# Causal attentions in tile order 3, 0, 2, 1, branch behind branch, the compressed branch folded into them, and finer waits at four stages

## What is computed

```python
def mla_mix(...):           # 12 heads, causal over 512 tokens
    s = einsum('bhqd,bhkd->bhqk', qb, k) * scale
    p = masked_softmax(s, key_pos <= tq);  o = einsum(p, v)
def nsa_mix(...):           # 12 heads in 2 groups, three branches
    s_c = einsum(qb, kc) * scale - m * dist_c        # 31 compressed keys
    p_c = masked_softmax(s_c, cmp_end <= tq);  o_c = einsum(p_c, vc)
    ...                     # o_s: top 16 of 8 blocks, so all of them; o_w: window of 512
    o = g0 * o_c + g1 * o_s + g2 * o_w               # g = sigmoid(gates)
def memory_attention(...):  # softmax over 256 memory positions
x = layer_norm(DN_ALPHA * x + concat([o_tok, o_mem]) @ w_out, ...)
```

## Time and profile before

| | |
|---|---|
| median of 3 runs | 3133.34 us (3130.97 to 3135.99) |
| the profiled execution's own time | 3133.84 us |
| its span, first to last instruction | 3132.0 us |
| mean granted TensorE clock | 0.985 |
| PE busy | 3007.3 us, 96% |
| DVE, ACT, POOL busy | 1258.7, 1072.1, 159.1 us |
| chain that ended last | PE 86%, DVE 8%, ACT 3%, issue 2% |

### The profile page before, as it was taken

How to read it: one execution, slowest core, us unless ns; L and a number is a source line. 1 busy time by engine, 2 the same in 40 slices (tenths; PEclk the granted TensorE clock), 3 DMA queues, 4 the chain that set the end, 5 groups by cost and what they waited for, 6 DMA issues and landing times.

```text
span 3132.0 us, 36507 instructions
## 1 busy us (share of the span) xinstructions
PE 3007.3 (96%) x15462; PEld 2505.1 (80%) x15462; DVE 1258.7 (40%) x1802; ACT 1072.1 (34%) x1856; POOL 159.1 (5%) x187
## 2 busy tenths in 40 slices
PE   8999999999999899999899999899999978999998
PEld 6888888888888788888668888788888855688887
DVE  3464344333335533325554322332332548543323
ACT  3323244443444322213653222212231227623221
POOL 1000000030001000001000000100000114000000
PEclk9999999999999999999999999999999969999999
DMA  5333232232221222223112332432322420023222
GB/s 198 124 105 95 99 102 77 85 89 88 74 87 49 94 94 94 94 96 114 43 42 81 95 108 94 110 108 93 96 94 94 118 53 2 28 94 94 94 96 80
DMA packets 135010, 280.06 MB, mean 89 GB/s; under 512 B 20378, under 2 KB 33098, under 8 KB 134720
## 3 DMA queue, kind: packets, MB, share of 16 engines
q1 hardware_dynamic: 125232, 247.17, 24.5%
q0 software_dynamic: 9616, 30.57, 3.2%
HBM read 271.30 MB, written 4.25 MB: 88 GB/s over the span
## 4 chain that ended last, share of the span: by engine, by line
PE 86%; DVE 8%; ACT 3%; issue 2%; DMA 1%; POOL 1%; SPq 0%; POOLq 0%; DVEq 0%; ACTq 0%
PE bank L535 24%; PE bank L537 24%; PE bank L536 23%; PE bank L691 2%; PE bank L670 2%; PE bank L546 1%; PE bank L548 1%; PE bank L549 1%; PE bank L724 1%; PE bank L743 1%; PE bank L732 1%; DVE n_p L1714 1%; PE bank L679 1%; DVE w_low L1530 1%; PE bank L651 1%
## 5 line engine op out<-in xcount | busy, mean ns | idle before, releaser
L1530 DVE TENSOR_TENSOR w_low<-raw,w_high 128x2048 fp32r<-128x2048 f32 (+3 forms) x214 | 483.8, 2261 | 1250.0 <-ACT w_high L1145 1243.7
L535 PE MATMUL bank<-xt_high,w_high 128*128 128x512 f32 x1984 | 779.1, 393 | 3.6 <-DVE w_low L1530 3.2
L537 PE MATMUL bank<-xt_high,w_low 128*128 128x512 f32 x1984 | 773.4, 390 | 0.0
L536 PE MATMUL bank<-xt_low,w_high 128*128 128x512 f32 x1984 | 772.7, 389 | 0.0
L1145 ACT ACTIVATE w_high<-raw 128x2048 fp32r<-128x2048 f32 (+3 forms) x214 | 404.1, 1888 | 933.8 <-PE bank L537 933.8
L535 PEld LDWEIGHTS bank<-xt_high,w_high 128*128 128x128 f32 x1984 | 372.2, 188 | 80.5 <-DVE w_low L1530 3.7
L537 PEld LDWEIGHTS bank<-xt_high,w_low 128*128 128x128 f32 x1984 | 372.1, 188 | 79.4
L536 PEld LDWEIGHTS bank<-xt_low,w_high 128*128 128x128 f32 x1984 | 372.4, 188 | 76.7
L535 PE MATMUL bank<-w_high,hidden_high 128*128 128x512 f32 x656 | 256.2, 391 | 3.1 <-DVE gate_rows L1899 3.1
L536 PE MATMUL bank<-w_low,hidden_high 128*128 128x512 f32 x656 | 255.5, 390 | 0.0
L537 PE MATMUL bank<-w_high,hidden_low 128*128 128x512 f32 x656 | 255.4, 389 | 0.0
(11 more groups left out here) (353 smaller groups left out, 4017.7 us busy)
## 6 DMA issues: line engine op xcount, KB each, us to landing
raw<-in_ffn_w_gu SPq DMA_DIRECT2D x80, 1024.0 KB, 5.1
raw<-in_ffn_w_down SPq DMA_DIRECT2D x44, 1024.0 KB, 5.0
raw<-in_b_w_in SPq DMA_DIRECT2D x40, 1024.0 KB, 5.1
raw<-in_a_w_in SPq DMA_DIRECT2D x24, 1024.0 KB, 5.2
raw<-in_a_w_out SPq DMA_DIRECT2D x8, 1024.0 KB, 5.0
raw<-in_ffn_w_gu SPq DMA_DIRECT2D x16, 512.0 KB, 4.5
raw<-in_w_out SPq DMA_DIRECT2D x5, 1024.0 KB, 5.1
raw<-in_w_mem_kv SPq DMA_DIRECT2D x4, 1024.0 KB, 5.3
```

Source lines behind the costliest of these rows:

```text
L535: pe.matmul(o, lh, rh, start=start, stop=False, skip_group_check=True)
L536: pe.matmul(o, lh, rl, start=False, stop=False, skip_group_check=True)
L537: return pe.matmul(o, ll, rh, start=False, stop=stop, skip_group_check=True)
L1530: dve.tensor_tensor(homes[n][1][:, 0:w], RAW[n % 2][:, 0:w], homes[n][0][:, 0:w].bitcast(F32), ALU.subtract).then_inc(sem["w_low_ready"], ...
```

## The change

1. **Order of tasks.** In both attentions the tiles of a pair come as 3, 0, 2, 1. In NSA the second branch's four tiles come behind the first's, and the memory tasks come first instead of last. POOL's release for the bias of pair i is moved with them.
2. **Compressed branch.** Its scores come ahead of the gates' product. Softmax runs on two tiles at a time, without the multiply by the mask (the maximum is held above NEG/2 instead), the exponentials of both halves before the first attention step, the rest beside the steps of the memory tasks (`compressed_beside`). The gates become exp on ACT and add, reciprocal on DVE. Its values are four products at the start of each pair into the pair's own bank; the copy to and the add from `cmp_o_t` go, and so do the waits on them. The split of the second w_out panel moves to steps 20 (ACT) and 22 (DVE).
3. **`free` by tile.** `down` calls `free(t)` ahead of each tile's first product: in gMLP, FFN and w_out. w_out waits for each pair's split where it uses it.
4. **b_gate and b_out.** `bgate_read` by tile. ACT does slots 8 and 9 and the group exponential ahead of the next weight panel, DVE the differences and slot 9. DVE splits b_out's second panel ahead of `merge(1, 3)`. b_out's last two panels and the first two of the FFN get homes without a wait.
5. **l02.** It gets a home for the last panel and the order of the other stages; POOL does its powers before the loads of the compression's weights, which wait for the last panel.
6. **bias_rows.** Its products come between the two panels of v 0, not behind them.

```diff
+    WIDE_FIRST = (3, 0, 2, 1)
@@ mla_tasks
-            for t in range(TT):
+            for t in WIDE_FIRST:
@@ nsa_tasks
+        mem_tasks(out, nQM, nKV)
         for i in range(HEADS // 2):
-            for t in range(TT):
-                for br in range(2):
+            for br in range(2):
+                for t in WIDE_FIRST:
                     for g in range(2):
...
-        return mem_tasks(out, nQM, nKV)
+        return out
@@ product
+                if between and i == 0:
+                    between()
@@ down
-            free()
             for i, g in enumerate(gs[:-2]):
...
                     for t in range(TT):
+                        if i == 0 and kk == 0:
+                            free(t)
@@ tensor: attend_pairs
+                    compressed = name == "nsa" and tasks[a]["pair"] < HEADS // 2
+                    if compressed and tasks[a]["opens"]:
+                        i = tasks[a]["pair"]
+                        for t in range(TT):
+                            pe.matmul(ps[tasks[a]["bank"]][:, t * P:t * P + P], VBD[:, i % 2, :], nCT[:, t, i // 2, :],
+                                      start=t == 0, stop=False, skip_group_check=True)
...
+                if beside:
+                    beside(u)
@@ tensor: ffn
+            def free(t):
+                if t == 0:
+                    pe.wait_ge(sem["gate_read"], at("gate_read", (f, 5, 1)))
+                if t == 1:
+                    pe.wait_ge(sem["up_read"], at("up_read", (f, 5, 1)))
@@ tensor: w_out
+            def free(t):
+                if t == 2:
+                    pe.wait_ge(sem["pt_copied"], at("pt_copied", (name, len(tasks) - 1)))
+                if t == 3:
+                    pe.wait_ge(sem["pair_split"], at("pair_split", (name, tasks[-1]["pair"])))
@@ tensor: nsa
+        def compressed_beside(u):
+            if u == 1:
+                pe.wait_ge(sem["gates_t_read"], at("gates_t_read"))
...
+            if 3 <= u < 7:
+                t = u - 3
+                pe.wait_ge(sem["cmp_p_ready"], at("cmp_p_ready", t // 2))
+                if t:
+                    pe.wait_ge(sem["cmp_pt_copied"], at("cmp_pt_copied", t - 1))
...
+            if u == 6:
+                pe.wait_ge(sem["cmp_pt_copied"], at("cmp_pt_copied", TT - 1))
@@ scalar: b_gate
-        for j in range(8):
+        for j in range(10):
             attend_slot(last, j)
-        prepare(ids["b_gate", 0][0] + 2)
         act.wait_ge(sem["group_diffs"], at("group_diffs"))
         act.activation(bE[:], bE[:], ACT.Exp).then_inc(sem["group_exps"], step("group_exps"))
+        prepare(ids["b_gate", 0][0] + 2)
@@ vector: attend_pairs
-                if 8 <= n < N + 8 and tasks[n - 8]["closes"] and name == "nsa" and tasks[n - 8]["pair"] < 6:
...
-                    dve.tensor_tensor(nOC[:, j, :], ps[tasks[n - 8]["bank"]][:], nOC[:, j, :],
-                                      ALU.add).then_inc(sem["pair_summed"], step("pair_summed", j))
@@ vector: b_out
         merge(1, 2)
+        prepare(ids["b_gate", 1][1] + 2)
         link(merge(1, 3))
-        dve.wait_ge(sem["bgate_read"], at("bgate_read", 1))
         for t in range(TT):
+            dve.wait_ge(sem["bgate_read"], at("bgate_read", (1, t)))
             gate(1, t)
-        prepare(ids["b_gate", 1][1] + 2)
@@ vector: compressed_beside
+            if n not in (4, 6):
+                return
+            half = (n - 4) // 2
...
+            dve.wait_ge(sem["cmp_exp"], at("cmp_exp", half))
+            link(dve.tensor_reduce(half_of(CSUM, half), p, AX.X, ALU.add))
...
+            dve.tensor_tensor(p, p, over_keys(CWGT, half), ALU.mult).then_inc(sem["cmp_p_ready"], step("cmp_p_ready", half))
@@ gpsimd
-        pool.wait_ge(sem["product_done"], at("product_done", ("panel", ids["down", 0, 1][-3])))
...
+        roots("l02")
+        pool.wait_ge(sem["product_done"], at("product_done", ("panel", ids["down", 0, 1][-1])))
         load(W1[0][:], A["cmp_w1_2"][0].rearrange("(k p) n -> p k n", p=P), "w1_loaded")
...
-        roots("l02")
```

More of the change, by code:

```diff
@@ L348, in build @@
         for i, (g, (high, low)) in enumerate(edge):
-            homes[g] = (at_off(f"edge_high_{s}_{i}", [P, 2048], rg + high * KB, F32R),
-                        at_off(f"edge_low_{s}_{i}", [P, 2048], rg + low * KB, F32R))
-            freed_by[g] = free
+            home(f"{s}_{i}", g, high, low)
+            freed_by[g] = ids[y][-5 if len(ids[y]) > 4 else -4]
+    for i, (g, high, low) in enumerate(zip(ids["b_out"][2:] + ids["gate", 0, 0, 0], (72, 48, 0, 24), (80, 64, 8, 32))):
+        home(f"s2_{i}", g, high, low)
     ring = [g for g in range(len(panels)) if g not in homes]
@@ L444, in dilated_tasks, with row_task @@
         return out
-    def row_task(out, q, k, scale, bias, W, v, pair, o, t, gate=None, first=True, last=True):
+    opened = []
+    WIDE_FIRST = (3, 0, 2, 1)
+    def row_task(out, q, k, scale, bias, W, v, pair, o, t, gate=None, first=True, last=True, tiles=range(TT)):
         n = len(out)
@@ L455, in row_task @@
         tk.update(bank=6 + pair % 2, rows=slice(o, o + 64), cols=slice(P * t, P * t + P), first=first, last=last,
-                  pair=pair, opens=o == 0 and t == 0 and first, closes=o == 64 and t == TT - 1 and last)
+                  pair=pair, opens=o == 0 and t == tiles[0] and first, closes=o == 64 and t == tiles[-1] and last)
+        if tk["opens"]:
+            opened.append(pair)
+        tk["behind"] = opened[-3] if tk["opens"] and len(opened) > 2 else None
         out.append(tk)
@@ L572, in edge_product, with product @@
             edge_part(second, 1, 1, jobs, ("acc", name))
[L574 removed]
+        def product(name, nk, jobs, free, between=None):
             gs = ids[name]
@@ L744, in attend_pairs @@
                                             PTs[m % 4][:, i * P:(i + 1) * P],
-                                            start=tk["first"] and i == 0, stop=tk["last"] and i == parts - 1)
+                                            start=tk["first"] and i == 0 and not compressed,
+                                            stop=tk["last"] and i == parts - 1, skip_group_check=compressed)
                             if i == parts - 1:
                                 ins.then_inc(sem["weighted"], step("weighted", (name, m)))
+                if beside:
+                    beside(u)
         def turn_half(c, t):
@@ L1259, in attend_pairs @@
                     j = tasks[n - 8]["pair"]
-                    if name == "nsa" and j < 6:
-                        act.wait_ge(sem["pair_summed"], at("pair_summed", j))
-                        src = nOC[:, j, :]
-                    else:
-                        act.wait_ge(sem["weighted"], at("weighted", (name, n - 8)))
-                        src = ps[tasks[n - 8]["bank"]][:]
-                    act.activation(HH[:, j, :], src, ACT.Copy).then_inc(sem["pair_high"], step("pair_high", (name, j)))
+                    act.wait_ge(sem["weighted"], at("weighted", (name, n - 8)))
+                    act.activation(HH[:, j, :], ps[tasks[n - 8]["bank"]][:], ACT.Copy).then_inc(sem["pair_high"], step("pair_high", (name, j)))
+                if beside:
+                    beside(n)
         first_rows()
```

281 lines of the change are left out of this document (123 added, 158 removed).

## The result

The changed kernel takes 3109.2 us (median of 4 runs, 3108.0 to 3111.5) against 3134.7 us (3131.0 to 3139.5) on the same chip: a ratio of 0.992, 95% interval 0.990 to 0.994. It is faster by 25.5 us, where I had forecast 59; the time lies above my range. The profiled execution has a span of 3106.6 us. Of the kernel best2 further down, the time is the median of three executions, since the fourth, the profiled one, took 10481.8 us; so none of its stages is read.

The account below looks back on a forecast made before the run. PE bounds the kernel, busy 96% of the span, leaving 125 us idle plus half-clock work to win. Terms -29.5 -2.1 -13.9 -10.6 -3.1 -0.7 +1.1 = -58.8 us give 3075 us, range 3057 to 3096.

Parts of the forecast that it names:

- NSA: Last attention, first memory score to w_out: 153.2 us against 182.7 before, -29.5, bounds -40 to -22.
- The memory phase: Start of NSA: eight memory steps of 14 us on PE plus softmax, gates, waits and slow clock, together 24 us.
- The pair: NSA head pair: 17.7 us of PE work plus stalls, 19.4; 20.7 beside POOL, first pair 22.6; bounds 17.7 to 21.7.
- Both signs of this: Signs the forecast is wrong: NSA pairs of 21 us or more, and a clock of 0.50 anywhere in pairs 1 to 5.
- The second term: NSA pairs while POOL writes the next bias: 1.25 us more each, taken from old pairs of 20.99 against 19.74.
- Rival (b): DVE limits the attentions, POOL's blocks falling on 512-key steps, 2.96 instead of 1.25 us a pair: 3090 us, chance 0.20.
- Rival (e): NSA pair stalls grow to about 2 us unbroken idle and the clock falls: 106 us more, 3181 us, chance 0.02.
- MLA: MLA attention: 0.2 us less in each of six pairs, a slower fill, earlier w_out: -2.1 us, bounds 1 and -4.
- Bias rows: Bias products moved earlier delay the last v tile by 1.35 us and win 0.29: +1.1 us.
- s2: Stage of b_gate and b_out: three PE idle spells and half clock behind them shrink, -13.9 us, bounds -8 and -17.
- l02 and the FFN before it: l02: idle before its transposes, following spells and half clock go, -10.6 us; FFN waits for up_read go, -3.1 in all.
- FFN and gMLP: FFN's four waits for up_read go, -3.1 us; gMLP's last wait goes likewise, -0.7 us.

Follow-up runs that it names:

- best2: best1 with POOL's attention-bias work halved by putting the causal mask into the distance table: 3058.2 us, ratio 0.976.
- Run 2, copy_first: Changed kernel with ACT's copy of the transposed tile issued ahead of the exponential in both causal attentions: 3092.6 us, ratio 0.987.
- runs 2 and 8: Changed kernel with ACT's copies ahead of its exponentials: 3092.6 us; the same with POOL making only the first two pairs' biases (work left out): 3075.8 us.
- best1: Changed kernel with NSA order 0, 1, 2, 3, MLA 1, 3, 2, 0, ACT's copies first, b_out's panel earlier, bias rows in the last banks: 3065.6 us.
- run 6: Changed kernel with POOL writing the biases of the first two head pairs only, the others reusing them (work left out): 3101.7 us, one run.
- run 9: Changed kernel with useless PE work added, each score product of a 128-key task made three times in both causal attentions: 3102.9 us, ratio 0.990.
- order_old: Changed kernel with both attentions' tiles back in order 0, 1, 2, 3 and NSA's branches alternating at each tile: 3085.2 us, ratio 0.984.
- order_seq: Changed kernel with both attentions' tiles in order 0, 1, 2, 3, NSA's branches still one behind the other: 3087.4 us, ratio 0.986.

## Why the prediction failed

By its own steps:

- **NSA, -29.5 forecast, -2.0 measured: 27.5 of the 33 us missed.** The memory phase was right in total (24 forecast, 22.8 measured). The pair failed, in one step: "for the steps of 128, 384 and 256 the same sum leaves PE as the later one". I summed PE and DVE only, and the trace has PE waiting 0.64 and 0.67 us for ACT's copies at the 256-key step, 0.65 at the 128-key one. ACT's copies and exponentials stood in my rows as busy time (15.3 of 20 us a pair), but I never laid its queue against PE's. Run 2 shows that its order costs 13.2 us. Both signs of this came: pairs of 21 or more, and a clock of 0.50 in pairs 1 to 5. The second term is POOL. I took 1.25 us a pair from a pair of the old order, in which POOL starts at a narrow step. With ACT's queue mended, it costs 3.1 to 3.5 us in the order 3, 0, 2, 1 (23.2 to 23.6 against 20.1, runs 2 and 8) and 1.8 in the order 0, 1, 2, 3 (best1, 21.04 against 19.26). Without both a pair is 20.1, against my 19.4. Taken by parts: first pair 29.1 (22.6), the next four 25.3 on average (20.7), last pair with drain 27.7 (23.8). In the first pair PE idles 2.04 us ahead of 2538.79, for a normalising of two memory tasks that took 2.01 beside POOL, and 2.54 ahead of 2547.84, for a copy that stands in ACT's queue behind the split w_high (1.90); the clock is at 0.50 from about 2536 to 2543.
- **Rival (b)** named POOL on the 512-key steps and priced it at 2.96 a pair instead of 1.25. That is near the 3.1 to 3.5 which POOL costs once ACT's queue is mended. But in the changed kernel itself POOL alone is worth 6.5 us in NSA, and of ACT the rival says nothing. POOL's writing costs 0.7 us a pair, like against like, where PE waits on ACT (run 6) and over 3 where it waits on DVE (runs 2 and 8). The Trainium skill (SBUF — State Buffer, section on SBUF's two separate sides) has a port pair that DVE and GpSimd share, as an exclusive lock for the whole instruction. The normalising of 2.77 us beside POOL and 1.00 alone fits that; no run here shows the lock itself.
- **Rival (e)**, the clock: it falls in each pair, from less than I set. Not one unbroken idle of 2 us but 1.03 and 0.35 with 0.44 of work between was followed by 0.50. My price of 106 us was wrong the other way: the half clock lasts 3 to 7 us a pair, and run 9 puts its worth behind the first pair at 4 us. The premise that the clock was 1.00 in every pair of the old order holds only behind the first, in which it stood at 0.50 until about 2581. That a kernel's clock falls back between bursts, as the Trainium skill says (TensorE: Matmul & The Clock Gate, on oscillation in real kernels), the trace now shows in the pairs of the changed kernel.
- **MLA, -2.1 forecast, +1.3 measured.** Pair 11.02 instead of my 10.5, by the same step: with ACT's queue turned it is 10.47. The start of w_out without the last split did come: order_old has the old pair and 82.0 against 83.5, -1.5 (forecast -1.45).
- **Bias rows, +1.1 forecast, +2.7 measured.** The wait is 2.75 us, as I wrote. What I left out is the clock behind it; 1.35 us more:
```profile
48.00:50.00 2.00, 2.00 (x6) 1.51 (x6) 1.56 (x1) 0.00 (x0) 1.15 (x3) 0.50 0.12 29
```
- **s2, -13.9 forecast.** From the dilated stage to MLA's input the shift goes from +1.7 to -11.7, thus 13.4, of which one FFN wait is 0.8: 12.6. The single steps: 980.06 gained 3.4 as forecast; the waits of 4.24 and 1.97 are gone. But b_out's first product waits 4.06 us, not the 2.3 that I had put there (1.30 as before and 1.0). PE, then DVE:
```profile
1020.13 0.47 PE L546 MATMUL bank<-w_high,b_y_high 128*128 128x512 f32 x1 [4.06 <-issue]
```
```profile
1015.77 2.06 DVE L1878 TENSOR_TENSOR b_y_low<-bank,b_y_high 128x512 fp32r<-128x512 f32 x2
1017.76 2.27 DVE L1555 TENSOR_TENSOR w_low<-raw,w_high 128x2048 fp32r<-128x2048 f32 x1
```
  The page says "issue"; the row of w_low, which ends at 1020.03, names the true releaser. It stands in DVE's queue behind a merge and two low halves; best1 moves it ahead, and 2.66 us of the wait go. The half clock behind it goes too, and best1's stretch from the last dilated step to MLA's first score is 5.7 us shorter. The sign "an idle over 3 us ahead of b_out" had come.
- **l02 and the FFN before it, -11.4 forecast, -11.8 measured** (-9.2 to -21.0). No idle stands before the transposes, and the edge wait is 0.59:
```profile
2011.71 1.04 PE L663 MATMUL bank<-ident,x_rows 128*128 128x128 f32 x8
...
2016.10 0.39 PE L557 MATMUL bank<-xt_high,edge_high_l 128*128 128x256 f32 x1 [0.59 <-DVE xt_low L1574]
```
  The compression's weights land in time: no new wait shows at its products.
- **FFN and gMLP**: the four waits of 0.78 and the one of 0.7 are gone, as forecast.

With NSA, MLA and the bias rows at their measured values my sum would be -58.8 + 27.5 + 3.4 + 1.6 = -26.3, against -25.4 of the span. (The pair's transposes and values stand in it at 5.3 and 5.6 us. By the stated rule, in proportion to the keys, they would be 5.2 and 5.1; the prediction does not show the rows that it took for narrow tiles. The 0.6 us are small beside the miss.) The range was too narrow because its bounds for a pair (17.7 to 21.7) came from the same sum of two engines.

What stays open: why an order is good or bad beside POOL is shown by totals and by pairs with and without it, not instruction by instruction; what share of the miss the half clock has apart from the idle time that brings it; and the first pair. From its first score to the next pair's it takes 29.1 us in the changed kernel, 27.9 in order_old, 27.3 in order_seq, 27.2 in copy_first and 22.5 in best1, where alone the clock is 1.00 throughout (0.88, 0.69, 0.87 and 0.87 in the others). So neither the order nor ACT's queue alone gives back what it lost, and 5.4 of the 9.3 us by which best1's NSA is shorter than order_old's lie in it.

## What to carry over

When steps of different width are reordered in a pipeline over three engines, lay out each engine's queue for one round, the copying engine too: a busy share of 75% says nothing of a copy that stands behind an exponential. Price a disturbance (POOL here) at the step on which it will fall, not by its average, and expect two causes on one chain to hide each other until both are gone. If a change of several parts gains less than reckoned, try the parts alone: here the order of the tasks took back 18 of the 20 us that the rest gave in NSA.

## What the runs showed of the hardware

The granted clock fell behind short idle spells that a little work separates (1.03 and 0.35 us), and filling them with useless products kept it at 1.00 behind the first pair and made the kernel 6 us faster. In the same round the spells of 0.64 and 0.67, with 0.41 of work between, were not followed by a fall.

It is not the same each time either. Before the product of MLA's latents PE idles 2.61 us in both kernels; behind it the clock is 0.50 in the changed kernel and 1.00 in the kernel before:
```profile
1472.00:1474.00 2.00, 2.00 (x6) 1.52 (x6) 0.87 (x6) 0.00 (x0) 0.00 (x0) 0.50 0.41 68
```
```profile
1484.00:1486.00 2.00, 2.00 (x10) 1.65 (x9) 0.60 (x4) 0.60 (x1) 0.00 (x0) 1.00 0.47 115
```
order_seq and order_old, whose code is the same up to there, start MLA at 1517.7 and 1520.4, the first without that fall, the second with it. So single marks carry some 1 to 3 us that no part of the change explains.
